# The last expert's gate folded into its rows, and the partial sums moved between VectorE's last low parts

## The reference, cut to what matters

```python
for e in range(N_EXPERTS):
    u = jax.nn.silu(t @ w_gate[e]) * (t @ w_up[e])
    out = out + gates[:, e:e + 1] * (u @ w_down[e])
...
y = layer_norm(ALPHA * h + f, ln2_g, ln2_b)      # f is out
```

## Time and profile before

| what | value |
|---|---|
| time, median of 3 runs | 1029.28 us (1028.82 to 1029.68) |
| the profiled execution's own time | 1029.47 us |
| its span in the trace | 1027.7 us |
| busy: PE, DVE, ACT, POOL | 97%, 77%, 47%, 37% of the span |
| granted TensorE clock | 0.993 of full speed |

### The profile page before, as it was taken

How to read it: one execution, slowest core, us unless ns; L and a number is a source line. 1 busy time by engine, 2 the same in 40 slices (tenths; PEclk the granted TensorE clock), 3 DMA queues, 4 the chain that set the end, 5 groups by cost and what they waited for, 6 DMA issues and landing times.

```text
span 1027.7 us, 19645 instructions
## 1 busy us (share of the span) xinstructions
PE 999.9 (97%) x7246; PEld 904.1 (88%) x7246; DVE 793.4 (77%) x982; ACT 478.5 (47%) x674; POOL 379.0 (37%) x278
## 2 busy tenths in 40 slices
PE   7999999999999999999999999998999999999995
PEld 7999999999999999999999999986677777777773
DVE  4598889888989985844434498237989898999987
ACT  4232322223232335134442323452788887878765
POOL 3444444444454755344544454320200000000355
PEclk9999999999999999999999999998999999999998
DMA  7432323233232222333235522647999999999475
GB/s 219 120 103 82 102 82 97 86 88 95 85 99 82 82 83 73 101 111 91 82 102 162 186 82 92 257 154 286 398 389 397 391 399 389 399 391 399 155 247 179
DMA packets 147290, 190.55 MB, mean 185 GB/s; under 512 B 6819, under 2 KB 114339, under 8 KB 147228
## 3 DMA queue, kind: packets, MB, share of 16 engines
q1 hardware_dynamic: 140107, 176.74, 49.4%
q0 software_dynamic: 3008, 10.55, 3.2%
q10 hardware_dynamic: 4129, 2.67, 0.9%
HBM read 179.16 MB, written 11.76 MB: 186 GB/s over the span
## 4 chain that ended last, share of the span: by engine, by line
PE 91%; DVE 5%; issue 2%; DMA 2%; ACT 1%; POOL 0%; SPq 0%; DVEq 0%; POOLq 0%; ACTq 0%
PE pr L1079 60%; PE pr L1269 16%; PE work L1269 8%; DMA sb_tok<-in_state_conv_b_dram 1%; PE work L1245 1%; PE work L1161 1%; PE pr L1310 1%; PE pr L1289 1%; DMA hs<-h_rows,ids 0%; PE work L1186 0%; DVE y_a L2015 0%; PE work L1087 0%; PE pr L1234 0%; DVE q_hi L1596 0%; PE pr L1178 0%
## 5 line engine op out<-in xcount | busy, mean ns | idle before, releaser
L595 POOL TENSOR_TENSOR w_lo<-raw,w_hi 128x512 fp32r<-128x512 f32 x208 | 297.2, 1449 | 326.8 <-ACT w_hi L724 326.8
L1079 PE MATMUL pr<-x_hi,w_hi 128*128 128x260 f32 x1264 | 255.2, 283 | 0.0
L1079 PE MATMUL pr<-x_hi,w_lo 128*128 128x260 f32 x1264 | 254.8, 283 | 0.0
L1079 PE MATMUL pr<-x_lo,w_hi 128*128 128x260 f32 x1264 | 254.3, 283 | 0.0
L728 ACT ACTIVATE ev<-pr 128x520 f32<-128x520 f32 x96 | 58.2, 606 | 372.7 <-PE pr L1079 372.7
L1079 PEld LDWEIGHTS pr<-x_hi,w_hi 128*128 128x128 f32 x1264 | 195.0, 189 | 0.3
L1079 PEld LDWEIGHTS pr<-x_hi,w_lo 128*128 128x128 f32 x1264 | 194.9, 188 | 0.0
L1079 PEld LDWEIGHTS pr<-x_lo,w_hi 128*128 128x128 f32 x1264 | 194.3, 188 | 0.0
L1522 DVE SCALAR_TENSOR_TENSOR work<-b_pad,par,work 128x512 f32<-128x512 f32 x224 | 148.1, 742 | 0.0
L724 ACT ACTIVATE w_hi<-raw 128x512 fp32r<-128x512 f32 x208 | 118.9, 622 | 3.7 <-DMA raw<-in_w_in_dram 3.4
L632 POOL DMA_INDIRECT hs<-h_rows,ids x15 | 19.3, 1288 | 247.5 <-DVE ids L1801 247.5
(11 more groups left out here) (397 smaller groups left out, 1749.7 us busy)
## 6 DMA issues: line engine op xcount, KB each, us to landing
raw<-in_w_in_dram SPq DMA_DIRECT2D x80, 512.0 KB, 3.7
w_gate<-in_expert_w_gate_dram SPq DMA_DIRECT2D x16, 2048.0 KB, 14.4
w_up<-in_expert_w_up_dram SPq DMA_DIRECT2D x16, 2048.0 KB, 13.0
w_down<-in_expert_w_down_dram SPq DMA_DIRECT2D x16, 2048.0 KB, 12.5
y_rows<-y_out SPq DMA_DIRECT2D x14, 384.0 KB
raw<-in_w_a_out_dram SPq DMA_DIRECT2D x8, 512.0 KB, 4.1
raw<-in_w_c_out_dram SPq DMA_DIRECT2D x8, 512.0 KB, 4.1
raw<-in_w_b_out_dram SPq DMA_DIRECT2D x8, 512.0 KB, 3.9
```

The lines of the kernel that those rows point to most:

```text
L595: pool.tensor_tensor(w_lo[:, slot, k], raw[:, slot, k], w_hi[:, slot, k].bitcast(F32), ALU.subtract).then_inc(w_split, 1)
L1079: mm = pe.matmul(pr[slot][:, h, 0:HALF], w[:, slot, k, :], x[:, k, h * HALF:(h + 1) * HALF], start=(k == 0 and w is w_hi and x is hi), sto ...
```

## The change

- The last expert's gate is no longer carried by the one-hot matrix. `weigh_last` (VectorE, at the start of the experts) splits it into three bf16 columns, which `find_ids` for that expert gathers with the token numbers; `last_gate_in` (ScalarE, step 13) adds them up in `last_gate`. `last_rows_out` multiplies by it, so the rows in DRAM carry the gate, and `share` is a plain matrix of 0 and 1 with no low part: two products for each half where there were three.
- `share_marks` and the small operations for `slot_ready` move up into step 15, ahead of the last expert's low parts, and the four transposes into the middle of its up product.
- `partial(0)` stands between the low parts of chunks 1 and 2, `partial(1)` behind that of chunk 3, `partial(2)` and `partial(3)` behind `share_low(1)`.
- Block 0 has no identity product: `others_first` adds `y_b[0]` to the partial sum on VectorE, between the two `share_low`, and `summed_up(0)` adds the result.
- GpSimd fetches blocks 0 and 1 of `y_b` before the sample rows of `y_a`, and blocks 2 and 3 behind them.
- ScalarE writes `y_last_hi` first, and writes `y_last` of a half only when VectorE has finished that half's `share_low` (`end_dve`). The Sqrt that loads the function table moves from before the branch to behind it.

The diff, cut to its core:

```diff
+            pool.wait_ge(slots_ready, 4)
+            pool.wait_ge(first.stored, 16 * E)
+            fetch(y_b, slot_ready, y_b_in, y_rows[0:(E - 1) * C, :], (0, 1))
+            pool.wait_ge(end_dve, 3)
             fetch_samples(sy_a, 0, y_a_in, y_rows[0:EARLY * C, :])
+            fetch(y_b, slot_ready, y_b_in, y_rows[0:(E - 1) * C, :], (2, 3))
...
             def last_rows_out(ps, t, q, row0):
+                act.wait_ge(ps.half_ready, q * 3 + 1)
                 for h in range(2):
                     act.wait_ge(ps.done["down"], t * CH + CH + 2 * (h + 1))
-                    act.activation(y_last[:, cols], work[0][0:C, h, :], ACT.Copy).then_inc(ps.half_ready, 1)
                     if ps is first:
-                        if h == 0:
-                            act.wait_ge(end_mm, 2)
-                            act.activation(share_hi[:], pr[1][0:C, 1, :], ACT.Copy).then_inc(end_act, 1)
-                        act.activation(y_last_hi[:, cols], work[0][0:C, h, :], ACT.Copy).then_inc(end_act, 1)
-                    act.wait_ge(ps.half_ready, q * 2 + (h + 1))
+                        act.activation(y_last_hi[:, cols], work[0][0:C, h, :], ACT.Copy, scale=last_gate[:]).then_inc(end_act, 1)
+                        act.wait_ge(end_dve, 4 + h)
+                    act.activation(y_last[:, cols], work[0][0:C, h, :], ACT.Copy, scale=last_gate[:]).then_inc(ps.half_ready, 1)
+                    act.wait_ge(ps.half_ready, q * 3 + (h + 2))
                     act.dma_start(y_rows[bass.ds(x * C + row0, C), cols], y_last[:, cols]).then_inc(ps.half_stored, 16)
...
-            act.activation(r_tok[0:1, 0:1], eps_t[0:1, 0:1], ACT.Sqrt)
             n_max = further_passes(act)
...
+            act.activation(r_tok[0:1, 0:1], eps_t[0:1, 0:1], ACT.Sqrt)
             normalised()
...
+                pe.wait_ge(partial_ready, 2)
+                others(1)
+                for h in range(2):
+                    pe.wait_ge(end_act, 2 + h)
+                    pe.wait_ge(end_dve, 4 + h)
+                    mm = own(0, h)
...
+            def weigh_last():
+                x = TURN[E - 1]
...
+                do(dve.tensor_tensor(s_t[:], own(oh1), s_w1[:], ALU.mult))
+                do(dve.tensor_copy(last_cols[:, :, 0:2], id_cols[:]))
+                step(dve.tensor_tensor(s_max[:], own(oh2), s_w2[:], ALU.mult))
+                step(dve.tensor_tensor(s_t[:], s_t[:], s_max[:], ALU.add))
+                for j in (2, 3):
+                    step(dve.tensor_copy(part(j), s_t[:]))
+                    step(dve.tensor_tensor(s_t[:], s_t[:], part(j), ALU.subtract))
+                do(dve.tensor_copy(part(4), s_t[:]), Tally(dve, bias_ready, 2))
...
+            def others_first():
+                dve.wait_ge(partial_ready, 1)
+                dve.wait_ge(y_b_in[0], 16)
+                do(dve.scalar_tensor_tensor(y_a[:, 0, :], y_b[:, 0, :], s_wm[:, 0:1], y_a[:, 0, :], ALU.mult, ALU.add))
```

More of the change, by code:

```diff
@@ L554, in _ @@
                 sp.wait_ge(partial_ready, NTB)
+                for b in range(4):
+                    sp.wait_ge(y_b_in[b], 16)
                 sp.wait_ge(end_mm, 6)
@@ L673, in _, with fetch @@
                                channel_multiplier=-1).then_inc(const_ready, 1)
-            def fetch(dst, slot, landed, table):
-                for b in range(4):
+            def fetch(dst, slot, landed, table, blocks=range(4)):
+                for b in blocks:
                     pool.indirect_dma_start(out=dst[:, b, :], out_offset=None, in_=table,
@@ L955, in step @@
                         tokens_in(ps, m + 1, t + 1)
+                    if m == 13:
+                        last_gate_in(ps, t + 2)
                     if m:
@@ L967, in expert_pass @@
                 rounded_parts(ps, "down", 0, uses[0] + 5, t, last=True, chunks=(0, 1))
+                if ps is first:
+                    act.wait_ge(end_mm, 1)
+                    act.activation(share[:], pr[1][0:C, 1, :], ACT.Copy).then_inc(end_act, 1)
                 u_in_last(ps, t, 0)
@@ L1344, in step @@
                         up_last(ps, t, 0, x_hi_t, x_lo_t)
+                        if ps is first:
+                            pe.wait_ge(end_dve, 1)
+                            for b in range(4):
+                                mm = pe.transpose(pr[1][0:C, 1, b * P:(b + 1) * P], share_tok[:, b, :], ident[:])
+                            mm.then_inc(end_mm, 1)
                         pe.wait_ge(ps.silu_ready, t + 2)
@@ L1370, in expert_pass @@
                 down_last(ps, t, 0, 1)
-                if ps is first:
-                    pe.wait_ge(end_dve, 3)
-                    for b in range(4):
-                        mm = pe.transpose(pr[1][0:C, 1, b * P:(b + 1) * P], share_tok[:, b, :], ident[:])
-                    mm.then_inc(end_mm, 1)
                 down_last(ps, t, 1, 1)
@@ L1790, in pick_weights @@
                 step(dve.tensor_tensor(s_w2[:], s_w2[:], s_sum[:], ALU.mult))
+            def weigh_last():
+                x = TURN[E - 1]
+                own = lambda t: t[:, :, x:x + 1].rearrange("p b o -> p (b o)")
+                part = lambda j: last_cols[:, :, j:j + 1].rearrange("p b o -> p (b o)")
+                do(dve.tensor_tensor(s_t[:], own(oh1), s_w1[:], ALU.mult))
[6 more added lines that the diff above has]
+                do(dve.tensor_copy(part(4), s_t[:]), Tally(dve, bias_ready, 2))
+                last[0] = chain
             def mark(ps, x):
@@ L1838, in expert_pass @@
                 take_ids(ps, 1, n0 + 1)
+                if ps is first:
+                    weigh_last()
                 if ps is further:
@@ L1886, in expert_pass @@
                 gated_part(ps, t, 1)
+                if ps is first:
+                    dve.wait_ge(back_in, 48)
+                    partial(0, 16)
                 low_parts(ps, "down", 0, t, (2,), last=True)
                 u_low_last(ps, t, 1)
+                if ps is first:
+                    spread_samples()
                 low_parts(ps, "down", 0, t, (3,), last=True)
                 if ps is first:
-                    spread_samples()
-                    share_marks()
-                    partials(16)
-            s_wa, s_wb = s_max, s_sum
+                    partial(1, 16)
+                    share_low(0)
+                    others_first()
+                    share_low(1)
+                    partial(2, 16)
+                    partial(3, 16)
+            s_wm = s_w2
             def find_slots():
@@ L1976, in share_low @@
                 dve.wait_ge(end_act, 2 + h)
[L1977 to L1987 removed]
+                dve.scalar_tensor_tensor(y_last_lo[:, cols], work[0][0:C, h, :], last_gate[:], y_last_hi[:, cols].bitcast(F32), ALU.mult,
+                                         ALU.subtract).then_inc(end_dve, 1)
             def partials_late():
[L1990 removed]
                 sample_partial(16)
@@ L2003, in summed_up @@
                     s = b % 2
-                    dve.wait_ge(y_b_in[b], 16)
+                    dve.wait_ge(y_b_in[b], 16 if late_partials else 32)
                     dve.wait_ge(end_mm, b + 3)
-                    step(dve.scalar_tensor_tensor(z_tile[b][:], wide(y_b[:, b, :]), s_wm[:, b:b + 1], z_tile[b][:], ALU.mult, ALU.add,
+                    others, weight = (y_a[:, 0, :], 1.0) if late_partials and b == 0 else (y_b[:, b, :], s_wm[:, b:b + 1])
+                    step(dve.scalar_tensor_tensor(z_tile[b][:], wide(others), weight, z_tile[b][:], ALU.mult, ALU.add,
                                                   accum_out=agg[:, s, 0:1]))
```

119 lines of the change are left out of this document (59 added, 60 removed).

## The result

| what | before | after |
|---|---|---|
| time, median of 21 runs each | 1028.68 us | 1030.81 us |
| ratio, 95% interval | | 1.0020 (1.0013 to 1.0027) |
| the profiled execution's own time | 1029.47 us | 1030.49 us |
| its span | 1027.7 us | 1028.8 us |
| granted TensorE clock | 0.993 | 0.991 |

The change costs 2.1 us, where I forecast 0.9 (1030.2 us): slower by the interval, and by about as much as I had called the smallest difference that tells (2.06 us), so "the same" held only just. The mechanism is the forecast's, but three of its terms were too small. The lower granted clock is not the cause: it is 1.00, the higher of its two levels, in both kernels from 745 to 1012 us and falls only behind that (to 0.75 before and 0.55 after), where TensorE has little left to do (4.45 and 1.17 us).

What follows compares the result with a forecast made beforehand. The last 50 us bound it: VectorE's sums and normalisations, started by the first normalisation, which ScalarE would delay. 1.06 - 0.15 = +0.91 on 1029.47 gives 1030.4; the median is 0.19 lower, so 1030.2 us, range 1028.3 to 1031.6.

Steps and rivals of the forecast that it cites:

- the band for ScalarE deciding: End of the kernel: the forecast's own mechanism, ScalarE setting the first normalisation, 1029.9 to 1031.0 us, chance 0.55.
- the small signs: Step-by-step signs in the tail, among them: VectorE idles about 0.5 before the second `y_last_lo`, none before `others_first`.
- rival 3: VectorE's exchange with ScalarE: `y_b[0]` comes late and holds `others_first`; 1030.5 to 1034.4 us, chance 0.1.
- ScalarE decides the first normalisation: Block 0's normalisation: it waits for ScalarE's Square and starts at 1012.37, 1.06 us later than before.
- Rival 1: ScalarE's branch: it costs less, so VectorE alone sets the normalisation, at 1009.8; 1027.6 to 1029.5 us, chance 0.2.
- Partial sums between the low parts: VectorE, last expert: `partial(0)` ahead of the third low part makes the last low part end at 999.43, 0.97 late.
- `last_gate_in` delays ScalarE in step 13 within the slack of a step whose chain is TensorE's; I cost them at nothing: ScalarE, step 13: reading the gate's columns, with `weigh_last` and the extra columns on VectorE, was costed at nothing.
- `order_slots`: Early part: two copies go, a cast and a wait come; 0 to 0.16 us, taken as 0.1.
- The copies at 0.59: ScalarE's copies of the last expert's rows: `y_last` was taken at 0.59 us, half 1 ending at 1004.84.
- The branch term: ScalarE from its last copy's end to the Square: 6.19 us as before, plus 0.1 to 0.16 for the small Sqrt.
- Rival 2: ScalarE in the exchange: the DMA issue doesn't hold it, `share_low(1)` comes 0.5 earlier; 1029.7 us, chance 0.1.
- 0.15 back at the third `summed_up`: VectorE behind the first normalisation: without TensorE to wait for, 0.25 becomes 0.1, so 0.15 us comes back.

Runs made afterwards that it cites:

- a1_arms: The changed kernel with ScalarE's two arms exchanged, so its branch is no longer taken: 1028.31 us, 0.9996 of the kernel before.
- c1_gate: The changed kernel with ScalarE's reading of the gate's columns (`last_gate_in`) moved from step 13 to step 14: 1031.03 us, a single time.
- c3_scale: The changed kernel with the gate left out of ScalarE's four copies of expert 15's rows: last copy ends 15.44 us behind `y_out`'s store; no run time given.
- c4_quiet: The changed kernel with the gathers of `y_b` for blocks 2 and 3 moved behind GpSimd's branch and the sample gather: 1030.43 us, a single time.
- e1_quiet_again: c4_quiet unchanged, run for a second trace: 1028.94 us, a single time.

## Why the prediction was right, and where its sizes were off

The time lies in the range 1028.3 to 1031.6 and in the band for ScalarE deciding (1029.9 to 1031.0). The three misses all went the same way, so none hid another. Two of the small signs failed: VectorE did idle before `others_first`, and it did not idle before the second `y_last_lo` (rival 3 below).

- **ScalarE decides the first normalisation.** Right: 3.31 us of idle on VectorE, released by ScalarE (forecast some 2.5), and a1_arms takes it away. Rival 1's end, VectorE alone, is the time of a1_arms: in the trace 1.5 us ahead of the kernel before, as rival 1 had it, in the median 0.4.
- **Partial sums between the low parts.** Right: the last low part ends 9.70 behind `y_out`'s store (998.44 less 988.74), before 8.91; forecast 0.87 more (0.97 less the 0.1 that falls ahead of the store), measured 0.79. `y_last_hi` of half 0 starts where forecast, 10.86 behind the store (forecast 1000.5 less 989.65, 10.85), but partly by luck: the low part came 0.08 sooner, and ScalarE's copy followed as much later.
- **"`last_gate_in` delays ScalarE in step 13 within the slack of a step whose chain is TensorE's; I cost them at nothing".** Wrong by 0.3 (c1_gate). The cover that I named was TensorE's, but VectorE, whose rows show no gap there, was the one that had none. With 0.1 forecast for `order_slots`, that is 0.2 to 0.3 missing in the sum.
- **The copies at 0.59.** Wrong by 0.10 each: they read the gate as an operand (c3_scale). `y_last_lo` on VectorE, which multiplies by the gate too, took 0.75 where 0.68 was forecast. The last copy ends 15.64 behind the store, forecast 15.19 (1004.84 less 989.65): 0.45, of which c3_scale gives back 0.2 before the gather takes its place.
- **The branch term, 6.19 + 0.1 to 0.16.** Measured 6.72, so 0.4 short. I had named `y_b`'s transfers as speaking for a shorter branch, as "y_b's transfers no longer run beside it". They did run beside it. The step that failed is rival 3's "so I take 4.2: 993.9". The size was close for the kernel before, where the store landed in 4.58; in the new order rows of `y_a` went ahead of it and it took 7.69. So the first gather was issued 8.45 behind that store's issue where I had 4.35, and the fetch of the code met the gathers (c4_quiet and its repeats).
- **Rival 3.** It came in a small degree: a wait of 0.64 for `y_b[0]`, hidden in the kernel after's two traces since `share_low(1)` had to wait for ScalarE anyway (1002.88 and 1002.91 lie together), and 1.0 us on ScalarE's path in c1_gate and c4_quiet. **Rival 2** fell: the DMA does stand ahead of the second `y_last_hi` (1001.82 and 1002.19).
- **0.15 back at the third `summed_up`.** Right: it comes 1.49 behind the normalisation (1013.87 less 1012.38), before 1.64.

In sum 0.91 forecast, and 0.2 + 0.45 + 0.4 missed, is 2.0 of the 2.1 us measured.

Expert 14's store landed 7.4 to 8.0 us behind its issue in all twelve traces of the new order, 4.6 and 4.8 in the two of the old. In the kernel before, GpSimd's second gather of `y_a` took 6.95 us to issue (983.28), so that two of the four came behind that store; after, all four are issued by 986.05 and their rows go ahead of it. No run changes that order alone, so it is read from the traces and not tried. What stays open is why that second issue took 6.95 us in both traces of the old order and takes 0.95 now.

## What to carry to other kernels

The branch that is taken over the block for further passes cost ScalarE 2.5 to 4.1 us here, and the longer times came with gathers on their way. Where one arm is the usual one, write it so that it falls through, as VectorE had it here, and see what engine stands closest to the end when covers are moved. An edit is only free if the engine that waits for it has slack, not the one that the profile shows as busiest; and a settling wait ahead of a branch exposes the reading of its register as well.

## What the runs showed of the hardware

- ScalarE's taken branch: 2.5 to 2.6 us without the gathers of blocks 2 and 3 in flight, 3.1 to 4.1 with them; not taken, the next instruction follows at once (a1_arms). The Trainium skill, page "Runtime: NRT & Kernel Launch", section "Instruction fetch mechanics", says that a taken branch whose target lies outside the fetched window waits for a DMA fetch of it; the packets of the instruction queue agree, and the runs give the price.
- A jump at the end of ScalarE's stream costs 3.3 us too (a1_arms, from the branch at 1022.28 to the next instruction at 1025.62, span 1025.9). The kernel after, without it, ends as late behind ScalarE's last DMA (1024.98 to 1028.8), since the last stores land then.
- A store that is issued behind gathers can wait for their rows: expert 14's moved nothing for 3.7 us with all four gathers of `y_a` ahead of it, and for 1.0 us where two of them were issued behind it (the kernel after and before).
- One issue of an indirect gather took 0.94 us in one execution of a kernel and 1.73 in another (e1_quiet_again, c4_quiet), and what it fetched landed later.
